# Gates computed inside the attention stage, turned probabilities copied ahead of the exponent, and weights laid by slice

## The reference

```python
a = rmsnorm(h, norm_mix);  z = a @ w_in                      # 1152 x 9240
y_m = mlstm_chunkwise(qm, km, vm, i_pre, log_fm, C, n, m)    # 4 heads of 256, state carried
log_ff = log_sigmoid(ff + b_f);  c = cumsum(log_ff)          # the gates: 16 heads
s = q @ k.T * DH_F ** -0.5 + c_query - c_key;  s = where(k_pos <= q_pos, s, -inf)
y_f = softmax(s) @ v                                         # forgetting attention, 16 heads of 64
merge = sig(gm) * (y_m @ w_br_m) + sig(gf) * (y_f @ w_br_f);  h = h + merge @ w_out
h = h + peer(rmsnorm(h))          # top 16 of 16384 experts in each of 8 heads
h = h + sig(rmsnorm(h) @ w_pg) * (p @ w_pp);  y = rmsnorm(h)
```

## Time and profile before

| | us |
|---|---|
| median of 3 runs | 5291.07 (5285.33 to 5294.82) |
| the profiled execution | 5289.55 |
| its span in the trace | 5287.7 |
| PE busy | 4532.9 (86% of the span) |
| DVE busy | 3088.6 (58%) |
| ACT busy | 965.1 (18%) |

### The profile page before, as it was taken

One profiled execution on the slowest core, in us unless ns is written; L12 is line 12 of the kernel. 1 busy time (PEld: TensorE's weight loads), 2 busy tenths in 40 slices (PEclk: granted clock), 3 DMA queues, 4 the chain that ended last, 5 costly groups with the idle time before them and its releaser, 6 DMA issues. The chain is left out here.

```text
span 5287.7 us, 47730 instructions
## 1 busy us (share of the span) xinstructions
PE 4532.9 (86%) x16510; PEld 2777.6 (53%) x16510; DVE 3088.6 (58%) x6265; ACT 965.1 (18%) x1797; POOL 1233.2 (23%) x970
## 2 busy tenths in 40 slices
PE   8999669979859999677787689946899999999989
PEld 5555445536535555356566455635455445545444
DVE  1000333214567677489888617589677777777742
ACT  1110321111100111144444311113100000000013
POOL 0000001200004444243343100000344444444410
PEclk9999878889979999777776699969999999999999
DMA  4332344467729999888888687735899999999951
GB/s 143 124 113 87 103 132 152 166 232 285 255 111 392 408 407 402 315 329 317 308 332 313 243 318 276 250 122 171 355 419 419 418 414 417 412 414 415 408 233 58
DMA packets 464418, 1478.71 MB, mean 280 GB/s; under 512 B 38146, under 2 KB 204850, under 8 KB 361298
## 3 DMA queue, kind: packets, MB, share of 16 engines
q0 software_dynamic: 119872, 824.76, 38.7%
q1 hardware_dynamic: 344338, 651.36, 34.3%
HBM read 1370.05 MB, written 115.38 MB: 281 GB/s over the span
## 5 line engine op out<-in xcount | busy, mean ns | idle before, releaser
L2252 POOL DMA_INDIRECT ex_uv<-in_uv,idx x768 | 1142.2, 1487 | 1898.0 <-DVE ex_acc L2309 1646.0
L2293 DVE CUSTOM_DVE_ANT_0 ex_uv<-ex_uv,ex_xp 128x1024 f32<-128x1024 f32 x768 | 915.4, 1221 | 350.3 <-DMA ex_uv<-in_uv,idx 304.7
L2309 DVE SCALAR_TENSOR_TENSOR ex_acc<-ex_uv,ex_wt,ex_acc 128x1024 f32<-128x1024 f32 x768 | 942.2, 1280 | 6.3
L2599 PE MATMUL exp_psum_dn<-exp_dn_big,exp_dn_gg 128*128 128x512 f32 x1536 | 683.4, 595 | 28.1 <-DVE exp_dn_gg L2521 28.1
L2590 PE MATMUL exp_psum_dn<-exp_dn_xT,exp_dn_big 128*128 128x384 f32 x2048 | 684.0, 488 | 13.3 <-DMA exp_dn_big<-in_ud 13.3
L386 PE MATMUL proj_psum_acc<-proj_w,aT_later 128*128 128x385 f32 x1920 | 624.8, 487 | 71.0 <-DMA proj_w<-in_w_in 64.3
L2590 PEld LDWEIGHTS exp_psum_dn<-exp_dn_xT,exp_dn_big 128*128 128x128 f32 x2048 | 390.4, 191 | 313.3 <-issue 62.4
L386 PEld LDWEIGHTS proj_psum_acc<-proj_w,aT_later 128*128 128x128 f32 x1920 | 363.9, 190 | 331.5 <-DMA proj_w<-in_w_in 64.5
L297 PE MATMUL proj_psum_acc<-proj_w,aT 128*128 128x385 f32 x1536 | 501.7, 488 | 5.0 <-DVE aT L230 2.8
L2599 PEld LDWEIGHTS exp_psum_dn<-exp_dn_big,exp_dn_gg 128*128 128x128 f32 x1536 | 290.4, 190 | 377.5 <-issue 350.8
L297 PEld LDWEIGHTS proj_psum_acc<-proj_w,aT 128*128 128x128 f32 x1536 | 291.0, 190 | 211.8 <-issue 4.4
(11 more groups left out here) (363 smaller groups left out, 4560.4 us busy)
## 6 DMA issues: line engine op xcount, KB each, us to landing
proj_w<-in_w_in SPq DMA_DIRECT2D x48, 1540.0 KB, 36.3
rt_w<-in_w_q SPq DMA_DIRECT2D x36, 2048.0 KB, 8.2
exp_dn_big<-in_ud SPq DMA_DIRECT2D x128, 512.0 KB
exp_dn_big<-in_vd SPq DMA_DIRECT2D x128, 512.0 KB, 8.1
scratch_z<-proj_zs SPq DMA_DIRECT2D x216, 192.5 KB, 2.2
rt_w<-in_w_br_m SPq DMA_DIRECT2D x18, 2048.0 KB, 10.0
rt_w<-in_w_br_f SPq DMA_DIRECT2D x18, 2048.0 KB
rt_w<-in_w_out SPq DMA_DIRECT2D x18, 2048.0 KB, 8.9
```

Source lines behind the costliest of these rows:

```text
L2252: pool.indirect_dma_start(self.uv[:, slot, :], None, self.uv_tab, bass.IndirectOffsetOnAxis(ap=self.idx[:, at:at + 1], axis=0)).then_inc(s ...
L2293: dve.tensor_tensor_reduce(self.uv[:, slot, 0:D], self.uv[:, slot, 0:D], self.xp[:], 1.0, 0.0, ALU.mult, ALU.add, self.dot[:, g % 2, j:j + ...
L2309: dve.scalar_tensor_tensor(out=self.acc[:, j % 2, :], in0=self.uv[:, slot, D:2 * D], scalar=self.wt[:, g % 2, j:j + 1], in1=self.acc[:, j ...
L2599: mm = pe.matmul(self.banks[t][:, n * 512:(n + 1) * 512], self.gg[:, 4 + q % 4, t * P:(t + 1) * P], self.big[:, 4 + q % 4, n * 512:(n + 1) ...
```

## The change

1. `stage_gates` is gone. Its work is the class `Gates`, called from `stage_attend`. SP issues the gate loads first, then the loads of `fx` and `ml`; then it waits for the sums, writes `nck`, waits for that to land, and issues the two `fkT` loads; then the copies to the outputs and, in the first stage, the sample gates' trip through DRAM. The scan for the samples and the write of `ncs` come after the last step. PE turns the gates after the first head's transposes. In the second stage the gates' buffers lie in `fprob`, `fprobT` and `fy`, and the turned gates in the scores' PSUM.
2. ACT copies the turned probabilities of s-1 ahead of exp(s), and does its `ml` slot ahead of both.
3. DVE does y(s-2) right behind max(s), in place of y(s-1) late in the step.
4. `w_in`, `w_br_m`, `w_br_f`, `w_out` and `w_q` are laid out by slice on the host, so that each partition reads one run of 12320 or 16384 bytes for a slice.
5. Two edits leave the program as it is at these sizes: `SBUFS` gives 2 and 1 as before, and the condition on `rides` holds for all of them.

```diff
 # stage_front, stage_project
-                sp.dma_start(w[:, u % U], w_in_v[:, :, u * CW:(u + 1) * CW]).then_inc(w_in_u[u % U], 16)
+                sp.dma_start(w[:, u % U].rearrange("p k n -> p (k n)"), w_in[u]).then_inc(w_in_u[u % U], 16)
 # stage_route
-            return w_out.rearrange("(k p) n -> p k n", p=P)[:, :, g * 512:(g + 1) * 512]
+            return w_out[g]
 # class FoxPrompt
     def sp_first(self, sp):
         for i in range(2):
             self.sp_qk(sp, i)
+            self.sp_v(sp, i)
+
+    def sp_sums(self, sp):
+        for i in range(2):
             self.sp_ck(sp, i)
-            self.sp_v(sp, i)
 # class Gates (what stage_gates did, in pieces)
+    def sp_sums(self, sp):
+        sp.wait_ge(self.summed, 2)
+        sp.dma_start(self.T["nck"][:, self.c0:self.c0 + self.NP], self.nck[:, 0:self.NP]).then_inc(self.nck_out, 16)
+        sp.wait_ge(self.nck_out, 16)
+    def pe_scores(self, pe):
+        pe.wait_ge(self.copied, 1)
+    def act_probs(self, act):
+        act.wait_ge(self.nck_out, 16)
 # stage_attend
         @block.sync
+            ga.sp_load(sp)
             fx.sp_first(sp)
             ml.sp_load(sp, 0)
             if ex:
                 ex.load_ahead(sp, g0)
+            ga.sp_sums(sp)
+            fx.sp_sums(sp)
+            ga.sp_rest(sp)
             for s in range(STEPS):
...
             ml.sp_last(sp)
+            ga.sp_last(sp)
         @block.tensor
             for g in range(len(fx.groups)):
                 fx.pe_head(pe, 0, g)
+            ga.pe_turn(pe)
+            ga.pe_scores(pe)
         @block.scalar
+            ga.act_first(act)
+            ga.act_probs(act)
             for s in range(STEPS + 1):
                 if s < STEPS:
                     for hd, g in fx.heads_at(s):
                         fx.act_head(act, hd, g)
-                    fx.act_exp(act, s)
                     ml.act_slot(act, *slot(s, 0))
                 if s >= 1:
                     for r in range(fx.rounds(s - 1)):
                         fx.act_probs(act, s - 1, r)
+                if s < STEPS:
+                    fx.act_exp(act, s)
         @block.vector
+            ga.dve_first(dve)
-            for s in range(STEPS + 1):
+            for s in range(STEPS + 2):
                 if s < STEPS:
                     fx.dve_max(dve, s)
+                if s >= 2:
+                    fx.dve_y(dve, s - 2)
+                if s < STEPS:
                     ml.dve_slot(dve, *slot(s, 0))
...
-                if s >= 1:
-                    fx.dve_y(dve, s - 1)
...
+            ga.dve_last(dve)
```

More of the change, by code:

```diff
@@ L1029, in stage_attend @@
+def stage_attend(nc, K, z, bias, cache_lf, gates, ck_last, C, m, T, b0, b1, ex=None, g0=0, g1=0):
     with Stage(nc, f"att{b0}") as st:
@@ L1031, in stage_attend @@
         ml = MlstmPrompt(nc, K, st, z, gates, C, m, T, b0, b1)
+        t0 = b0 + 1 if b0 else 0
+        ga = Gates(K, st, z, bias, cache_lf, gates, ck_last, T, t0, b1 + 1 - t0, fx)
         STEPS = fx.STEPS
@@ L2915 @@
     cols = lambda v: c(v.reshape(KD, P).T)
+    slices = lambda v, width: c(v.reshape(KD, P, -1, width).transpose(2, 1, 0, 3)).reshape(-1, P, KD * width)
     laid = dict(
@@ L2918 @@
         pT=c(np.concatenate([I["p_sample"].reshape(NSEQ * DSEQ, -1), I["p_prompt"].reshape(SEQ, -1)]).T),
-        norm_mix=cols(I["norm_mix"]), w_in=I["w_in"][0],
+        norm_mix=cols(I["norm_mix"]), w_in=slices(I["w_in"][0], CW),
         gate_bias=np.concatenate([I["mlstm_b_i"], I["mlstm_b_f"], I["fox_b_f"]], axis=1),
```

199 lines of the change are left out of this document (99 added, 100 removed).

## The result

The kernel after takes 5207.35 us (median of 4 runs, 5198.18 to 5214.43) for 5289.83 us before: a ratio of 0.9843, 95% interval 0.9825 to 0.9861. Its profiled execution took 5206.98 us with a span of 5205.2 us. The forecast was 5220 us, with 5195 to 5244 as its own range and 5175 to 5262 as the range of the whole prediction.

What follows compares the result with a forecast made beforehand. No single engine bounds the whole: PE limits the second projection and first attention stage, DVE the second attention stage. Gains of 24 + 31 + 11 + 5 = 71 us gave a median of 5220 us, range 5175 to 5262.

Steps and rivals of the forecast that it cites:

- gates: Ahead of both attention stages: first scores 18.1 and 22.3 us after the first gate load, 24 us won in sum.
- second order: Second attention stage: new ACT and DVE order removes DVE's 36.5 us ahead of fy, less 5 us new waits; 31 won.
- first order: First attention stage: the same orders cut PE's 33.2 us wait to 22 us, 11 us won.
- weights: Second projection and route stages: loads by slice win 5 us, a third of a 15 us bound.
- More goes than I count: Rival, 15%: half the Gelu's wait, the first stage's whole wait and 10 us more from weights go too; 5172 us.
- the Gelu takes the place: Rival, 14%, second attention stage: the Gelu, now behind the exponent, delays DVE up to 57 us; 5248 at half.
- one score buffer: Rival, 5%, second attention stage: the mix doesn't hide under the exponent, the stage takes 826 us; whole 5311.
- the gates are not hidden: Rival, 7%, ahead of the attention stages: SP's ring holds the nck write so long that nothing is won; 5244 us.
- the drain: Rival, 2%, second attention stage: a table switch costs unseen time in the chain, so the stage wins nothing; 5251 us.
- Slower: Rival, 5%: second attention stage 60 us longer if the mix isn't hidden; decides against the change from 10.1 us a step.
- PE's wait near 22 us: Sign for the first attention stage: PE's wait of 33.2 us falls to about 22 us, 48 waits of 0.46 us.
- the gates wait for the loads: Reason given for the gates' lower bound of 0 us won, ahead of the attention stages.

Runs made afterwards that it cites:

- e4: Kernel after with ACT's order alone put back (exponent ahead of slot and copies), DVE's new order kept: 5271.2 us, ratio 0.9970.
- e3: Kernel after with both old orders put back, on ACT and on DVE; gates under the loads and weights by slice kept: 5255.2 us, ratio 0.9942.
- e5: Kernel after with DVE's order alone put back (y of the step before at the end of a step), ACT's new order kept: 5183.6 us, ratio 0.9796.
- e12: Kernel after with one swap on DVE, y(s-2) directly ahead of max(s) instead of behind it: 5189.7 us, ratio 0.9804.
- e6: Kernel after with the gates' two ACT steps moved ahead of the scaling of the first heads: 5208.0 us, ratio 0.9838.
- e7: Kernel after; on DVE, group weights directly following their last dot product, and the half step's rest, deferred behind next slot or maximum: 5195.2 us, ratio 0.9816.
- e8: Kernel after with the loads of fv and of the first mLSTM tile issued behind the sums' write and the fkT loads: 5211.5 us, ratio 0.9854.
- e10: Kernel after with the gates' ACT steps ahead of the heads and the fv and mLSTM tile loads behind the sums: 5208.3 us, ratio 0.9850.
- e2: Kernel before, old weight layout, with 8 zs buffers for 5 in the second projection: 5294.1 us, ratio 1.0008.
- e1: Kernel before with only the weights' layout changed to by slice, for all five weights: 5277.8 us, ratio 0.9989.

## Why the prediction was right, and where it was not

**The sum.** 71 us were forecast against the profiled time, 82.6 came. Term by term: gates 24 forecast, 14.8 + 8.8 - 2.1 = 21.5 measured; second order 31, measured 29.6; first order 11, measured 18.5; weights 5, measured 9.0 in the second projection. Smaller shifts elsewhere (first projection 0.9, sample stage 2.5, both route stages and what follows them) make up the rest. "More goes than I count" came in part: the Gelu's wait stayed, PE's wait in the first stage went to 27.7 us and not to none, and the second projection gave 9.0 of the 15 us. The rivals "the Gelu takes the place" (33.5 us of wait for 32.2), "one score buffer", "the gates are not hidden" and "the drain" did not come about. "The drain" was also priced against its own numbers: a chain of 731 us is still under the 765.7 us that the stage took, so it would not have meant that nothing is won.

**The second stage: right size, wrong hand.** Nearly every sign that was named came: the stretch at 736.1 (730 to 740), the Gelu near 32, `fprobT` at 15.7 us (20 to 40), the new wait of the scores for `fprob`. But the step "With y(s-2) behind max(s), its mix is a step old, and the 36.5 us of DVE's wait go" gives the gain to the wrong edit. e4 has that edit without ACT's and is slower by 8.7 us in the stretch than e3, and e5 has ACT's without it and has hardly a wait ahead of `fy` either (2.9 + 2.1 us). The wait on DVE was a symptom: the copies of a step stood behind the exponent of the next, and with them the mix and the next scores. The prediction had written down this chain as the reason for PE's 150.6 us, and then counted the cure on DVE. It also took the new place of y as free. It cost 24 us in the whole (e5), 17.6 of them by standing behind rather than ahead of the maximum (e12), and its sign in the profile, 76.0 us of PE's mix for `fy`, was not forecast. "Slower" had been within reach only from 10.1 us a step; e4, at 780.8 / 80 = 9.8, shows that a kernel with half of this change would have come near it.

**The first stage: the wait about right, the rest luck.** For "PE's wait near 22 us" the kernel after has 24.3 us for the copies and 3.4 for `fy`, 27.7 in all. The 33.2 us that it was to come down from are read in a window that ends at 742 us; over the whole stretch, to 754.75, the wait was 37.1 us. So it fell by 9.4 us where 11 were forecast, and PE's idle time in the stretch by 6.7 us (38.5 to 31.8). The step that failed is the one that takes PE's work as given. The matmuls are the same 858, and yet PE's busy time went from 153.5 to 141.7 us, at a granted clock of 0.95 for 0.88: 11.8 of the 18.5 us. This part is not the order's alone. e6 has the orders of the kernel after too:

```profile
546.40:728.90 182.50, 153.58 (x858) 126.52 (x858) 79.32 (x286) 83.24 (x226) 0.00 (x0) 0.87 0.28 83
```

PE's work is there what it was before, 153.6 us, and the stretch is 9.5 us shorter, near the 11 of the sum. The five kernels with these orders (after, e6, e7, e8, e10) took 173.5 to 186.2 us, 180.1 in the mean, which is 11.9 under 192.0; the five with ACT's old order took 189.7 to 194.1. So some 7 of the 18.5 us are the luck of one profile.

**The gates: the number right, half of the reason.** The `nck` write was thought to land with the ten loads: 18.1 and 22.3 us. These are to the tenth what e6 shows, where the sums are early, and the tenths are luck: the write landed after 16.5 and 20.9 us (15.6 and 19.8 in the sum), the scores followed 1.6 and 1.5 us later (2.5 in the sum). In the kernel after ACT ended later than the queue, by 1.2 us in each stage: "the gates wait for the loads" stood among the bounds, and it was in fact ACT behind the heads, which wait for `fq` and `fk`. The step that failed is "Their arithmetic stays; it was ready 9.5 us after the first gate load": in its new place the negated sums were ready, and the write issued, only after 16.3 us. The sentence on SP, "the loop's first load is needed some 20 us later, so nobody waits", held here: the `fkT` loads went out 20.4 us after the first scores, behind the trip of `lfT`, and the third head's scores did not wait. (PE's one unnamed wait for scores in this stage, 1.9 us, comes at a later head, 64.5 us after the first scores.) There was little room to spare, as e8 and e10 show. The 2 us for the sample scan at the end of the first stage came as 2.1:

```profile
720.35 0.28 DVE L585 TENSOR_SCALAR att_fy<-att_psum_fy,att_finv 128x64 f32<-128x64 f32 x1 [2.40 <-issue]
720.55 1.25 DVE L1022 TENSOR_TENSOR_SCAN att_gcsum<-att_gone,att_gcs 128x528 f32<-128x528 f32 x1
...
725.99 0.33 SPq L1200 DMA_DIRECT2D smp_svc<-scratch_z  x1
```

5.36 us lie between the last y and the sample stage's first load, for 3.2 before.

**The weights: under-sized, and by its own test wrong.** It said that a projection moving by over 5 us would show it wrong, and the second one moved by 9.0: PE's 6.7 us behind ACT went whole, 1.2 us at the first slice and 1.4 at the drain of the last stores. The step that failed is "Each of these waits ends with another transfer or another engine close behind, so I take a third of the bound"; the 9.0 us are more than the 6.7 that its bound allowed a projection. e2 shows that there was such a transfer, a slice of weights 6.4 us late, but with the new layout both went together. In the route stages, which had been counted too, PE's two waits for `w_br_m` went from 8.7 to 7.5 us, and the first of these stages moved by 1 us.

The Trainium skill, page "Perfetto Trace Analysis", section "DMA Optimizations", promises dramatically better throughput for larger transfers. The landing of a slice agrees (36.3 to 13.1 us), while the stage gained 1.4%. The drain that the Trainium skill, page "ScalarE: Activation LUTs", section "What ACT_TABLE_LOAD costs", adds to a switch is again in no row: the load at 537.51 ends at 538.79 and the next ACTIVATE starts at 538.80.

## What to carry to other kernels

A wait tells who is late, not whom to reorder: follow the ring (here maximum, exponent, copies, mix, scores) once round and take out of it the piece that need not be in it; here an edit at the engine that waits only moved the wait (e4). When a change has two halves that both claim the same wait, price each alone, since one of them may be a cost. Where a start-up is shortened, look for the second thing that ends at the same time, and for every load that stands on the issuing engine behind a wait that was moved.

## What the runs showed of the hardware that was not expected

**The granted clock moved a stage by as much as the change did.** Two neighbouring windows of the first attention stage in the kernel before, and in e5 the ones at the same place (20 to 32 us after the first scores):

```profile
582.80:588.80 6.00, 3.63 (x24) 3.13 (x23) 2.81 (x10) 4.22 (x8) 0.00 (x0) 1.00 0.01 3
588.80:594.80 6.00, 5.43 (x21) 4.36 (x20) 2.16 (x7) 1.24 (x4) 0.00 (x0) 0.50 0.12 32
```

```profile
566.50:572.50 6.00, 5.05 (x30) 4.18 (x31) 3.98 (x15) 5.78 (x10) 0.00 (x0) 1.00 0.26 69
572.50:578.50 6.00, 4.54 (x28) 3.64 (x27) 2.52 (x10) 2.59 (x9) 0.00 (x0) 1.00 0.43 115
```

After a stretch in which PE had worked 3.63 of 6 us, it ran at 1.2 GHz: 5.43 us for 21 matmuls. In e5 it had worked 5.05 us in the window ahead and kept 2.4 GHz: 4.54 us for 28 (the matmuls of the two windows are not the same ones). That is no rule for when the clock falls. Later in the same trace of the kernel before, PE worked less still, and the clock stayed:

```profile
616.80:622.80 6.00, 3.54 (x26) 2.80 (x24) 2.00 (x8) 2.02 (x7) 0.00 (x0) 1.00 0.87 239
622.80:628.80 6.00, 4.34 (x30) 3.49 (x29) 1.53 (x7) 2.27 (x8) 0.00 (x0) 1.00 0.98 319
```

Nor does less idle time over the stage mean a higher clock: e6 had 28.9 us of it at a clock of 0.87, the kernel after 31.8 us at 0.95. What the clock costs is plain: the same 858 matmuls took 140.3 us at 0.97 (e5), 141.7 at 0.95, and 153.5 at 0.88. This is how one order gave 173.5 and 182.5 us in two kernels. In the second stage PE's work went from 600.9 us (0.71) to 572.6 (0.74) from the kernel after to e5. Whether the clock shortened that stage or only followed from it isn't settled, since DVE is its limit.

**A small write landed late while loads issued ahead of it were under way.** 24 KB took 4.4 us from issue to landing behind ten loads of the attention (e6) and 1.5 us behind four (e10), issued 12.1 and 12.0 us after the first gate load. In e10 the four were done by then, so the runs don't say whether it was the place in the queue or the traffic as such.

**The length of a DMA's rows showed in the transfers beside it.** With rows of 12320 for 1540 bytes, ACT's waits for a store of `zs` to land (206.2 us, 32 times) were gone in the second projection of e1 and of the kernel after, though the stores were the same. Whether it was the transfers or SP's shorter issues stays open.
